# Second block of a two-block layer: normalising queries and keys of tiles 0 to 2 while the experts' rows are still running, and projecting each tile ahead of its two norms

## The reference

```python
def peer(h, ...):            # per token: 128 indices idx, gates g = softmax(scores)
    z = jnp.einsum('td,thkd->thk', xc, u_experts[idx])
    return jnp.einsum('thk,thkd->td', gelu(z) * g, v_experts[idx])
x = x + gate2 * peer(h2, ...)
x = rmsnorm(x, final_g)                                # end of block 1
h = rmsnorm(x, attn_norm_g); proj = h @ w_in           # block 2, 1024 -> 2304
qa, ka, va, qb, kb, vb = split(proj)                   # 512,128,128,512,512,512
qa, ka = rope(rmsnorm(qa, gq_a)), rope(rmsnorm(ka, gk_a))   # norms over 64 elements
qb, kb = rmsnorm(qb, gq_b), rmsnorm(kb, gk_b)
out_a = softmax(qa ka^T / 8) va                        # 8 heads, 2 of keys
ob = (softmax(q1 k1^T / 8 + bias) - lam * softmax(q2 k2^T / 8 + bias)) vb   # 4 pairs
x = x + concat(out_a, norm(ob)) @ w_out;  x = x + relu(rmsnorm(x) @ w_up)**2 @ w_down
```

## Time and profile before

| | |
|---|---|
| median of 3 runs | 2331.58 us (2331.51 to 2332.46) |
| profiled execution: its own time | 2332.91 us |
| profiled execution: span from first to last instruction | 2331.1 us |
| busy over the span: PE, DVE, ACT, POOL | 2093.4, 1301.9, 918.3, 973.9 us |
| mean granted clock of TensorE | 0.968 |
| last row's products end | 1687.9 us into the span |
| first scores of attention start | 1746.1 us |
| first product of the MLP starts | 1976.9 us |

### The profile page before, as it was taken

The page is one execution under the profiler, slowest core; times in us unless marked ns, Lnnn a source line. Parts: engine busy times, 40 slices in busy tenths (PEclk is TensorE's granted clock), DMA queues, the critical chain, the costliest instruction groups (busy, mean ns, idle before and its releaser), DMA issues. The chain is left out here.

```text
span 2331.1 us, 21752 instructions
## 1 busy us (share of the span) xinstructions
PE 2093.4 (90%) x6824; PEld 1148.7 (49%) x6824; DVE 1301.9 (56%) x2997; ACT 918.3 (39%) x2346; POOL 973.9 (42%) x591
## 2 busy tenths in 40 slices
PE   7899998899998888986899989999878998999999
PEld 5687643333333333332333333333235554888887
DVE  5133456777778777785744454444467563432432
ACT  2453524444445444453333353333334442321321
POOL 0694004666664666653576766677510000000000
PEclk9999899999999999998999999999988998999999
DMA  9443428999999999999999999999820002232231
GB/s 369 146 145 106 147 109 360 420 414 417 417 412 390 421 417 403 422 396 417 419 416 422 417 418 399 410 421 421 365 98 31 1 1 74 90 109 91 91 109 55
DMA packets 118021, 651.67 MB, mean 280 GB/s; under 512 B 10872, under 2 KB 29200, under 8 KB 46096
## 3 DMA queue, kind: packets, MB, share of 16 engines
q0 software_dynamic: 73728, 536.90, 56.0%
q1 hardware_dynamic: 41232, 108.04, 12.9%
q10 hardware_dynamic: 2944, 5.33, 0.6%
HBM read 648.13 MB, written 2.10 MB: 279 GB/s over the span
## 5 line engine op out<-in xcount | busy, mean ns | idle before, releaser
L852 PE MATMUL bank<-ring,diag 128*128 128x512 f32 x2048 | 996.5, 614 | 147.3 <-ACT diag L1341 145.2
L543 POOL DMA_INDIRECT ring<-in_uv,idx x512 | 829.2, 1620 | 643.9 <-PE bank L852 232.7
L1887 DVE CUSTOM_DVE_ANT_0 zjunk<-ring,h 128x1024 bf16<-128x1024 f32 x512 | 627.2, 1225 | 456.3 <-DMA ring<-in_uv,idx 456.0
L852 PEld LDWEIGHTS bank<-ring,diag 128*128 128x128 f32 x2048 | 368.6, 191 | 712.3 <-ACT diag L1341 428.2
L1335 ACT ACTIVATE zg<-z 128x1 f32<-128x1 f32 x512 | 103.5, 202 | 702.1 <-DVE z L1887 701.6
L1341 ACT ACTIVATE diag<-ident,weight 128x128 f32<-128x128 f32 x512 | 205.5, 401 | 16.8
L818 PE MATMUL bank<-w_inb,hTb 128*128 128x512 f32 (+1 forms) x320 | 146.2, 559 | 0.7 <-ACT hTb L1329 0.7
L2101 DVE TENSOR_TENSOR ml_lo<-mlp_raw,ml_hi 128x2048 fp32r<-128x2048 f32 x32 | 73.4, 2293 | 114.4 <-ACT ml_hi L1483 114.4
L785 PE MATMUL bank<-w_q,h2T 128*128 128x512 f32 x256 | 130.0, 599 | 3.6 <-ACT h2T L1255 3.6
L1483 ACT ACTIVATE ml_hi<-mlp_raw 128x2048 fp32r<-128x2048 f32 x32 | 61.1, 1908 | 121.8 <-PE bank L575 107.6
L573 PE MATMUL bank<-hTm_hi,ml_hi 128*128 128x512 f32 x256 | 100.9, 394 | 1.6 <-DVE hTm_lo L2096 1.6
(11 more groups left out here) (247 smaller groups left out, 2590.9 us busy)
## 6 DMA issues: line engine op xcount, KB each, us to landing
ada_w<-in_w_ada SPq DMA_DIRECT2D x24, 1024.0 KB
mlp_raw<-in_w_up SPq DMA_DIRECT2D x16, 1024.0 KB, 5.5
mlp_raw<-in_w_down SPq DMA_DIRECT2D x16, 1024.0 KB, 5.0
win_raw<-in_w_in SPq DMA_DIRECT2D x9, 1024.0 KB, 6.2
w_inb<-in_w_in SPq DMA_DIRECT2D x8, 1152.0 KB, 26.5
w_q<-in_w_query SPq DMA_DIRECT2D x8, 1024.0 KB, 8.7
ring<-in_uv,idx POOLq DMA_INDIRECT x512
x<-in_x SPq DMA_DIRECT2D x8, 512.0 KB, 7.7
```

The lines of the kernel that those rows point to most:

```text
L543: e.indirect_dma_start(ring[n % RING], None, a["uv"], bass.IndirectOffsetOnAxis(ap=idx[i][:, j:j + 1], axis=0)).then_inc(s[f"d_ring{n % RI ...
L852: t = e.matmul(bank[2 * (i % 2) + half], diag[n % 4], ring[n % RING][:, 1024 + 512 * half:1536 + 512 * half], start=(j == 0), stop=(j == 127))
L1887: e.tensor_tensor_reduce(out=zjunk, in0=ring[n % RING][:, 0:1024], in1=h2[:, i, :], scale=1.0, scalar=0.0, op0=ALU.mult, op1=ALU.add, accu ...
```

## The change

- **Head norms beside the rows.** Keys and queries of tiles 0 and 1 and keys of tile 2 are squared, summed, rooted, scaled and roped by ACT and DVE in steps of the row loop, from rows 369, 436 and 464 on (`heads_behind`). All multiplies are DVE's; POOL has no head norms any more. Behind the rows remain tile 2's queries and tile 3's keys, and beside attention tile 3's queries.
- **Projection ahead of the norms.** `after_gather(i)` adds the gated sum to `x` by halves and multiplies each half by `slot[0]` = `attn_norm_g` x `final_g` (formed once at row 100); the product is transposed and projected at once. The two sums of squares (now DVE's, on `x`) and two roots come behind it; the product of the two factors, one number a token, multiplies the projection's result as the scale of ACT's copy out of PSUM.
- **Placing woven in.** PE transposes keys 0, 1, 2, queries 0, keys 3, queries 1 behind the five groups of `project2(3)`, through banks 0 and 1. `last_queries` holds only tiles 2 and 3, at units 0 and 11.
- **Transfers and places.** `rope` and a `gain` of 256 instead of 1664 columns (128 KB) are loaded beside the rows, behind the last `p_cmp`; the bias of head 0 (448 KB) behind the last row, of heads 1 to 3 behind the last projection. `rqk[3]`, the squares and the rope buffers move.

```diff
+HEADS2 = [(i, lo, hi) for i in range(NT) for lo, hi in ((16, 26), (0, 16))]
+HEADS_AT = {369: 0, 436: 1, 464: 2}
...
-        rqk = [tile(f"rqk_{n}", kb, 1664) for n, kb in enumerate((68, 74.5, 180, 16))]
+        rqk = [tile(f"rqk_{n}", kb, 1664) for n, kb in enumerate((68, 74.5, 180, 52))]
...
-        sq = slot[4]
...
+        sq = slot[1]
...
+        rot = [[slot[1][:, 512 * n:512 * n + 512] for n in range(2)], [tile(f"rot_{n}", 59 + 2 * n, 512) for n in range(2)]]
...
-        bias2 = tile("bias_rel", 140, 4 * 896).rearrange("p (h j) -> p h j", h=4)
+        bias2 = [tile(f"bias_rel_{h}", 140 + 3.5 * h if h else 63, 896) for h in range(4)]
...
+            q.wait_ge(s["p_cmp"], 16)
+            e.dma_start(rope, a["rope"].rearrange("i p c d -> p i c d")).then_inc(s["d_b2"], 16)
+            e.dma_start(gain.rearrange("p a d -> p (a d)"), a["gain_qk"].partition_broadcast(128)).then_inc(s["d_b2"], 16)
             q.wait_ge(s["p_acc"], 512)
-            e.dma_start(rope, a["rope"].rearrange("i p c d -> p i c d")).then_inc(s["d_b2"], 16)
-            q.wait_ge(s["v_ag"], 28)
-            e.dma_start(gain, a["gain_qk"].partition_broadcast(128)).then_inc(s["d_b2"], 16)
+            e.dma_start(bias2[0], a["bias_2"][0]).then_inc(s["d_bias2"], 16)
             q.wait_ge(s["p_pr2"], 20)
-            e.dma_start(bias2, a["bias_2"].rearrange("h p j -> p h j")).then_inc(s["d_bias2"], 16)
+            for h in range(1, 4):
+                e.dma_start(bias2[h], a["bias_2"][h]).then_inc(s["d_bias3"], 16)
...
-            head_norm(1)
-            head_norm(2)
-            head_norm(3)
...
-                    q.wait_ge(s["a_hT2"], 2 * i + 2)
...
+                        q.wait_ge(s["a_hT2"], 2 * i + 1 + k // 4)
...
-                for _ in range(8):
+                yield
+                for g in (0, 1):
+                    q.wait_ge(s["v_ag"], 12 * i + 3 * g + 3)
+                    if i < 3:
+                        q.wait_ge(s["a_hT2"], 2 * i + g)
+                    elif g:
+                        q.wait_ge(s["a_pr2"], 18)
+                    turn4(bank[7 if i == 3 and g else 5], slot[1], range(4 * g, 4 * g + 4)).then_inc(s["p_hT2"], 1)
...
+            for n, _ in enumerate(project2(3, [1] * 8)):
+                if n == 7:
+                    place_keys(0)
+                if n == 15:
+                    place_keys(1)
+                if n == 23:
+                    place_keys(2)
+                    place_queries(0)
+                if n == 31:
+                    place_keys(3)
+                if n == 39:
+                    place_queries(1)
...
+                for _ in range(11):
...
+                q.wait_ge(s["v_ag"], 12 * i + 12)
...
+                b, normed_by = bank[project_bank(c)], stats[:, 46 + i:47 + i]
...
+                    e.activation(rqk[i][:, lo:end], b[:, 0:end - lo], ACT.Copy, scale=normed_by).then_inc(s["a_pr2"], 1)
...
-                for step, ss in ((0, stats[:, 16 + i:17 + i]), (2, stats[:, 20 + i:21 + i])):
-                    q.wait_ge(s["v_ag"], 7 * i + (3 if step == 0 else 5))
-                    q.wait_ge(s["a_ag"], 4 * i + step)
-                    e.activation(t2, x[:, i, :], ACT.Square, accum_out=ss).then_inc(s["a_ag"], 1)
-                    yield
...
+                yield
+                yield
                 for g in (0, 1):
                     q.wait_ge(s["p_hT2"], 2 * i + g + 1)
                     q.wait_ge(s["v_z"], 128 * i + 128)
-                    e.activation(hT2[i][:, 4 * g:4 * g + 4, :], bank[5].rearrange("p (k q) -> p k q", k=4), ACT.Copy).then_inc(s["a_hT2"], 1)
+                    e.activation(hT2[i][:, 4 * g:4 * g + 4, :], bank[7 if i == 3 and g else 5].rearrange("p (k q) -> p k q", k=4),
+                                 ACT.Copy).then_inc(s["a_hT2"], 1)
+                    yield
+                for step, ss in ((0, stats[:, 16 + i:17 + i]), (1, stats[:, 20 + i:21 + i])):
+                    q.wait_ge(s["v_ag"], 12 * i + (10 if step else 7))
+                    e.activation(ss, ss, ACT.Sqrt, bias=eps, scale=1.0 / D).then_inc(s["a_ag"], 1)
+                    for _ in range(4):
+                        yield
+            def head_square(n):
+                i, lo, hi = HEADS2[n]
+                q.wait_ge(s["a_pr2"], 6 * i + (6 if lo == 0 else 3))
+                q.wait_ge(s["p_hT2"], 4 if n < 2 else 6 if n < 5 else 8)
...
+                e.activation(sq[:, 0:64 * (hi - lo)], rqk[i][:, 64 * lo:64 * hi], ACT.Square).then_inc(s["a_hs"], 1)
...
+            def head_root(n, part):
+                q.wait_ge(s["v_hs"], n + 1)
+                e.activation(part, part, ACT.Sqrt, bias=eps, scale=1.0 / 64).then_inc(s["a_rr"], 1)
...
+            def heads_behind(i):
+                head_square(2 * i)
+                yield
+                if i < 2:
+                    head_square(2 * i + 1)
+                    yield
+                yield
+                if i < 2:
+                    head_root(2 * i + 1, rr[:, i, 0:26])
+                else:
+                    head_root(2 * i, rr[:, i, 16:26])
                 yield
...
+            head_square(5)
+            project2_out(3, 0)
+            head_root(5, rr[:, 2, 0:16])
+            place_keys(0)
+            project2_out(3, 1)
+            head_square(6)
+            place_keys(1)
+            head_root(6, rr[:, 3, 16:26])
+            project2_out(3, 2)
...
+            project2_out(3, 3)
+            place_keys(3)
+            project2_out(3, 4)
+            place_queries(1)
...
-                yield from head_norms()
+                head_square(7)
+                yield
+                yield
+                yield
+                head_root(7, rr[:, 3, 0:16])
+                for _ in range(7):
+                    yield
...
-                t2, b = slot[1], 7 * i
+                t3, b = slot[1], 12 * i
                 ssf, ssa = stats[:, 16 + i:17 + i], stats[:, 20 + i:21 + i]
+                row = 128 * i + 132
                 q.wait_ge(s["p_acc"], 128 * (i + 1))
                 q.wait_ge(s["a_shift"], 16)
...
                 for half in (0, 1):
-                    e.tensor_tensor(t2[:, H[half]], bank[2 * (i % 2) + half], slot[3][:, H[half]], ALU.mult).then_inc(s["v_ag"], 1)
-                yield
...
-                for _ in range(41):
+                    cols, c = H[half], b + 3 * half
+                    e.tensor_tensor(t3[:, cols], bank[2 * (i % 2) + half], slot[3][:, cols], ALU.mult).then_inc(s["v_ag"], 1)
+                    q.wait_ge(s["v_ag"], c + 1)
+                    e.tensor_tensor(x[:, i, cols], x[:, i, cols], t3[:, cols], ALU.add).then_inc(s["v_ag"], 1)
+                    q.wait_ge(s["v_ag"], c + 2)
+                    e.tensor_tensor(t3[:, cols], x[:, i, cols], slot[0][:, cols], ALU.mult).then_inc(s["v_ag"], 1)
                     yield
+                for step, ss in ((0, ssf), (1, ssa)):
+                    c = b + 6 + 3 * step
+                    q.wait_ge(s["v_z"], min(row + 2 + 4 * step, 512))
+                    e.tensor_tensor_reduce(out=zjunk, in0=x[:, i, :], in1=x[:, i, :], scale=1.0, scalar=0.0,
+                                           op0=ALU.mult, op1=ALU.add, accum_out=ss).then_inc(s["v_ag"], 1)
+                    q.wait_ge(s["v_ag"], c + 1)
+                    yield
+                    yield
+                    yield
+                    q.wait_ge(s["a_ag"], 2 * i + step + 1)
+                    e.reciprocal(ss, ss).then_inc(s["v_ag"], 1)
+                    q.wait_ge(s["v_ag"], c + 2)
+                    if step == 0:
...
+                        q.wait_ge(s["v_ag"], c + 3)
+                    else:
+                        e.tensor_tensor(stats[:, 46 + i:47 + i], ssf, ssa, ALU.mult).then_inc(s["v_ag"], 1)
+                    yield
...
+            def head_sums(n):
+                i, lo, hi = HEADS2[n]
+                q.wait_ge(s["a_hs"], n + 1)
+                e.tensor_reduce(rr[:, i, lo:hi], sq[:, 0:64 * (hi - lo)].rearrange("p (h d) -> p h d", d=64), AX.X, ALU.add).then_inc(s["v_hs"], 1)
...
+            def head_scales(r, n, part):
+                i, lo, hi = HEADS2[n]
+                q.wait_ge(s["a_rr"], r + 1)
+                e.reciprocal(part, part).then_inc(s["v_rr"], 1)
+                if lo == 0:
+                    q.wait_ge(s["v_rr"], SCALED2[n] - 1)
+                    e.tensor_scalar(rr[:, i, 0:16], rr[:, i, 0:16], 0.125, None, ALU.mult).then_inc(s["v_rr"], 1)
...
+                qk = rqk[i].rearrange("p (h d) -> p h d", d=64)
+                q.wait_ge(s["v_rr"], SCALED2[n])
+                e.tensor_tensor(qk[:, lo:hi, :], qk[:, lo:hi, :], rr[:, i, lo:hi].unsqueeze(2).to_broadcast([128, hi - lo, 64]),
+                                ALU.mult).then_inc(s["v_kn"], 1)
...
+                if lo:
+                    for kind, h0, h1 in ((2, 16, 18), (3, 18, 26)):
```

(47 more changed lines are left out.)

312 lines of the change are left out of this document (114 added, 198 removed).

## The result

The changed kernel takes 2321.89 us (median of 5 runs, 2319.01 to 2324.44) against 2332.46 (2331.51 to 2339.48) of the kernel before on the same chip: a ratio of 0.9947, 95% interval 0.993 to 0.9965, which is some 12 us (the two medians lie 10.6 apart). A second comparison gave 2319.12 against 2336.57: 0.9917 (0.9902 to 0.9932), some 19 us. I had predicted 2307.8, a gain of 23.8, and a range that ends at 2320.

What follows compares the result with a forecast made beforehand. Transfers set the rows; a serial 58.2 us piece precedes attention. Savings 8.5 + 5.4 - 0.6 + 8 + 2.5 = 23.8 take 2332.91 to 2309.1, less 1.33 to the median: 2307.8 us; range 2298 to 2320.

Steps and rivals of the forecast that it cites:

- Part 1: Last row to first product: half-tile multiplies, transposes and projection ahead of the norms save 8.5 us, bounds 7.9 to 8.8.
- Part 2: First product to scores: all PE's own work, 39.3 us against 44.7, a saving of 5.4 us.
- the clock's term: First product to scores: 1.7 us charged for PE's clock falling, between 0 (no fall) and 3.4 (6.8 us at half clock).
- The `lam` exp: Before attention's first maxima: its table load starts only behind ACT's last query copy, charged 0.6 us.
- Rival D: DVE and ACT finish tile 3's keys late, so PE waits 5 us more: 2312.8, perhaps 2316; chance 0.04.
- Part 3: Attention's first tile: gaps between combines shrink toward 8.0 us, returning 8 of 12 us; bounds 0 and 12.
- rival A: Attention returns nothing: PE's fill or a tile-change stall brings clock 0.50 back; 2315.8 us, chance 0.16.
- Part 4: Row loop: tile changes, new roots, head work and extra transfers together gain 2.5 us, bounds -13 and +8.
- The third change: Row loop, third tile change: ACT's 4.23 us wait goes; 2.7 of 3.1 us lost transfer returned.
- the new roots: Row loop: three roots, each with two table loads, cost 0.3 us together; bound -9.3.
- Rival B: Row loop fuller than it looks: roots and DVE's 2.8 us meet used-up ring slack; -13.1, 2323.4 us, chance 0.10.
- C: Beside the rows, DVE work blocks POOL's gather descriptors, so 32.5 us of it is lost transfer; 2343.7 us, chance 0.04.

Runs made afterwards that it cites:

- values last: Changed kernel with tile 3's queries projected ahead of its values, the queries' norm beside the values' products; 2312.15 us, ratio 0.9886.
- the combined kernels: Changed kernel, tile 3's values projected after its queries, tile changes one pass a row: 2308.28 us; also heads' roots merged: 2310.48; or second squares a row later: 2309.43.
- the changed order: Profiled executions of the changed kernel (twice) and of experiments on it that leave the compared stage alone; the changed kernel took 2321.89 and 2319.12 us.

## Why the prediction was right and wrong

*Part 1, last row to first product: right.* 8.5 us for 8.5.

*Part 2, first product to scores: the right mechanism, a term too large.* 37.6 us for 39.3. In the profiled execution the products took 32.0 on the chain, 1.0 of it clock (7.87 for the first sixteen, 6.88 for others of their kind); I had 31.4 and 1.7. One pair of copies stood bare for 1.2 where I had 0.9. The 36 transposes were charged 5.3, at 0.146 each, a mean that held waits; on the chain they took 0.11 to 0.14, and some stood beside the copies. The 3.4 that bounds the clock's term stands in no row of the trace before; there the clock fell 4.4 us behind PE's last product (1687.9 to 1692.3), not 4.8. The `lam` exp was charged 0.6, and the first combine came 0.7 earlier: its table load (1737.14) lies beside the first scores. Rival D was wrong by far: tile 3's keys were roped at 1718.3, PE asked for them at 1728.5.

*Part 3, attention: the step that failed.* "DVE gives up rope of tiles 1 and 2 (2 x 2.3) and takes over two multiplies of tile 3 (2.4)" counted VectorE's work over the whole tile, and the prediction took 8 of the 12 us by which the gaps exceed 8.0 as what would return; 1.5 did. The wait for tile 3's rope did go (14.5 to 10.3). Two things took its place. The norm now sits in the first three gaps, where DVE's work and ACT's square and root stand between a maximum and its combine: at equal clock it costs 2.4 to 3.6 us (values last, 47.1), by the estimate above about half of it VectorE's multiplies and rope. And "the fall of the clock to 0.50 behind it" did not go: in the changed kernel PE stands at half clock behind the first combine, in the second gap and again in the fifth (1745, 1757 and 1785), and 8.5 to 10.2 us of clock are lost there as against 9.1 to 12.2 before; the combined kernels, which reach 44.9 to 43.7, lose 3.4 to 5.1. So rival A's number was right, 0 to 2 us of the 8, and so was its sign, clock 0.50 in the first units. That PE's pipeline fill brings it is not shown, and A has no word of the norm.

*Part 4, rows: wrong in sign, 4.2 us.* The third change gave 2.3 for 2.7. The bytes were charged 0.9, which no run takes by itself; with it the sum closes. For the first two I had returned 0.5 each; they cost 0.9 and 0.5. DVE was at 8.15 of 10 there and got 2.8 us more; ACT's saved squares were worth nothing beside that. And 0.1 for each of the new roots priced the wrong instruction: the roots are nearly free, but the square ahead of one, waiting on DVE in a queue that also feeds PE, cost 1.6 us on average at row 369. The view that would have warned me was in the earlier trace rows: PE busy for 54.9 of 60 us. I read DVE and ACT in that line and took their 1.3 and 1.5 us free a row for the slack of the stage, when the engine with the least had 0.2 us a row. Rival B's direction was right; C did not occur: its 32.5 us of new DVE work beside the rows cost 1.7 in all.

Sum of the misses: 6.5 in attention and 4.2 in the rows lost, 2.8 gained between rows and attention (1.5 of it in part 2, 1.3 with `lam`): 7.9 less than forecast, so 16. That 2.8 is luck as far as the time goes: terms set too large made up for a quarter of what the other two parts had wrong. That the first comparison shows 12 and the second 19 is within what single runs wander.

What stays open: why two of the fourteen executions with the changed order had late gathers ahead of row 436; why the fourth gap is 9.4 in every kernel with the changed order, with the norm or without, where it was 8.65 in two of three executions before; and what fixes the clock's pattern, in the first units and in the last 170 us of attention, which ranged from 168.8 to 176.5 with the same code there.

## What to carry to other kernels

Price a moved block by what stands behind it in each queue it enters, not by its own length: here a 1.06 us square that waited 2.9 cost more than two table loads, and a norm that was free under a projection cost 2.4 to 3.6 us between maxima and combines at equal clock. Compare stages at equal lost clock before a difference is put down to an edit. Before calling work hidden in a loop bound by transfers, take the slack from the busiest engine, and look whether its idle gaps drop its clock. An independent product (here the values) belongs last, so that the norm of what was projected ahead of it has a cover.

## What the runs showed of the hardware

The granted clock decided the same program both ways. PE idled for 2.04 to 2.73 us between two busy stretches at row 369 in nine executions with the roots. In six of them the clock fell to half and its next four products took 2.57 to 3.59 us instead of 1.98 (3.59 behind an idle of 2.63, 3.34 behind 2.04); in three, behind 2.05, 2.06 and 2.73, it did not. At full speed PE had 0.7 us of 10 to spare, so a wait with a fall lost 1.2 to 3.0 us of transfer, one without at most 0.9. In attention the same code took 222.7 to 228.2 us; the two executions at 228.2 lost 28 us of clock there, the others 21 to 23. And the table pair on ScalarE inside the chain of waits, 1.28 us twice, was worth 0.2 us when taken away, 0.6 to 1.3 at equal lost clock: being on that chain in one execution did not make it a cost of its length.
